# A two-block transformer kernel on one core: state-space products in another order, two tables awaited at first use, and squares ahead of tiles of h

## The reference, cut to what matters

```
# both blocks: mixing and the entry of the feed-forward part
o = merged @ w_out
x = x + g1 * rms_norm(o, g_post_mix)              # second block: x = x + o
h = rms_norm(x, g_pre_ffn) * (1 + sc2) + sh2
f = square(relu(h @ w_ff1)) @ w_ff2
# second block, state-space part, per group of 16 channels with 64 complex states
state[b] = decay * state[b-1] + inputs[b]         # b: blocks of 8 tokens, 128 of them
y[b] = C * state[b-1] + T * u[b]                  # T: lags inside a block of 8 tokens
y = gelu(y)
```

## Time and profile before

| what | us |
|---|---|
| runs: median (lowest to highest) | 3034.39 (3029.42 to 3040.65) |
| the profiled execution's own time | 3021.66 |
| its span, first to last instruction | 3019.9 |
| TensorE busy in the span | 2831.3 |
| VectorE, ScalarE, GpSimd busy | 1938.8, 1307.0, 235.5 |

### The profile page before, as it was taken

The page is one execution under the profiler, slowest core; times in us unless marked ns, Lnnn a source line. Parts: engine busy times, 40 slices in busy tenths (PEclk is TensorE's granted clock), DMA queues, the critical chain, the costliest instruction groups (busy, mean ns, idle before and its releaser), DMA issues. The chain is left out here.

```text
span 3019.9 us, 45306 instructions
## 1 busy us (share of the span) xinstructions
PE 2831.3 (94%) x18392; PEld 2252.8 (75%) x18392; DVE 1938.8 (64%) x2907; ACT 1307.0 (43%) x1908; POOL 235.5 (8%) x427
## 2 busy tenths in 40 slices
PE   7999858898999999989999999998899999999998
PEld 4776734577788788867778788887677888878886
DVE  7768888656776466784777524655646567655676
ACT  3026955457655434453441113222323565543344
POOL 0003620001100000000000001110000010000000
PEclk9999879999999999999999999998999999999999
DMA  7520100235666788731453331114224556667884
GB/s 251 173 84 29 36 1 1 84 112 174 216 224 233 280 259 298 254 120 53 136 161 125 122 110 52 57 48 117 105 91 146 187 196 226 234 247 262 287 296 155
DMA packets 195950, 471.31 MB, mean 156 GB/s; under 512 B 31584, under 2 KB 60384, under 8 KB 189408
## 3 DMA queue, kind: packets, MB, share of 16 engines
q1 hardware_dynamic: 178848, 392.94, 39.4%
q0 software_dynamic: 16896, 75.51, 6.2%
HBM read 344.09 MB, written 124.29 MB: 155 GB/s over the span
## 5 line engine op out<-in xcount | busy, mean ns | idle before, releaser
L2079 PE MATMUL psum<-merged_operand 128*128 128x512 f32 x1536 | 362.5, 391 | 5.8 <-ACT h_half L2332 5.8
L2079 PEld LDWEIGHTS psum<-merged_operand 128*128 128x128 f32 x1536 | 289.4, 188 | 67.6 <-issue 6.6
L2079 PE MATMUL psum<-h_half_operand 128*128 128x512 f32 x1344 | 316.8, 391 | 0.0
L2079 PEld LDWEIGHTS psum<-h_half_operand 128*128 128x128 f32 x1344 | 252.3, 188 | 55.5 <-issue 1.0
L2079 PE MATMUL psum<-h_half_operand,weight_parts_operand 128*128 128x512 f32 x768 | 180.0, 395 | 8.1 <-DVE weight_parts_operand L2564 4.1
L2079 PEld LDWEIGHTS psum<-h_half_operand,weight_parts_operand 128*128 128x128 f32 x768 | 144.5, 189 | 42.7 <-DVE weight_parts_operand L2564 7.3
L235 DVE CAST weight_high<-weight_ring 128x1024 fp32r<-128x1024 f32 (+1 forms) x64 | 37.9, 592 | 196.6 <-PE psum L3508 105.3
L3508 PE MATMUL psum<-h_high,weight_high 128*128 128x512 f32 x480 | 151.8, 397 | 1.4 <-DVE h_low L248 1.4
L3508 PE MATMUL psum<-h_low,weight_high 128*128 128x512 f32 x480 | 148.0, 390 | 0.0
L3508 PE MATMUL psum<-h_high,weight_low 128*128 128x512 f32 x480 | 147.9, 389 | 0.0
L2564 DVE TENSOR_TENSOR weight_parts_operand<-weight_ring,weight_parts_operand 128x1024 fp32r<-128x1024 f32 x66 | 80.7, 1223 | 94.4 <-ACT weight_parts_operand L2228 94.0
(11 more groups left out here) (614 smaller groups left out, 6218.4 us busy)
## 6 DMA issues: line engine op xcount, KB each, us to landing
o<-in_w_ff SPq DMA_DIRECT2D x80, 512.0 KB, 4.5
merged<-hidden_terms SPq DMA_DIRECT2D x56, 512.0 KB, 5.8
hidden_upper<-in_w_ff_down SPq DMA_DIRECT2D x48, 512.0 KB, 4.5
weight_ring<-in_w_out SPq DMA_DIRECT2D x32, 512.0 KB, 3.6
hidden_terms<-weight_parts POOLq DMA_DIRECT2D x16, 1024.0 KB, 7.7
hidden_terms<-weight_ring POOLq DMA_DIRECT2D x16, 1024.0 KB, 7.6
hidden_upper<-in_w_ff_up SPq DMA_DIRECT2D x32, 512.0 KB, 4.6
o<-hidden_terms SPq DMA_DIRECT2D x28, 512.0 KB, 6.0
```

Of the source, the lines that this page charges most:

```text
L2079: mm = pe.matmul(bank, w[:, at:at + P], tiles(r, i), start=opens and m == 0, stop=closes and m == 2, skip_group_check=resumed)
```

## The change

The diff has these parts.

- In `rwkv_output` the landings of `table` and `q` are counted on semaphores of their own; the block's last wait no longer counts them. VectorE waits for `table` ahead of its first use in `ssm_blocks`, TensorE for `q` ahead of its first use.
- The closing `stay_busy` of that block goes from 26 products to 10.
- In `ssm_blocks`, `outputs` becomes `add_inputs` (all products of `u_by_block` with `toeplitz`, opening the sums, ahead of `turn_y` of the four before) and `add_states` (the states' products: first the real parts, then the imaginary parts, each awaited by itself; in each, four of g = 0 and then four of g = 1). ScalarE copies bank 4 after g = 0's last product and bank 5 after g = 1's.
- In mixing with `first`, ScalarE's square of output tile 15 moves ahead of `round_h(5)`, and `keep_p1(0)` ahead of `round_h(6)`; VectorE's additions of squares 14 and 15 move ahead of `scale_first_h(4)` and behind `rest_of_first_h(4)`.
- In both calls `keep_p1(0)` waits for 15 added squares and no longer for 16.

```diff
@@ mix_and_ffn, keep_p1 @@
-                        wait(act, mix_added, MIX)
+                        wait(act, mix_added, MIX - 1 + m)
@@ ScalarE @@
                 if first:
-                    for k in range(4, KT):
-                        round_h(k)
+                    round_h(4)
                 square_output(MIX - 1)
+                if first:
+                    round_h(5)
+                    keep_p1(0)
+                    round_h(6)
+                    round_h(7)
...
-                    if m < PAIRS:
+                    if m < PAIRS and not (first and m == 0):
                         keep_p1(m)
@@ VectorE @@
+                if first:
+                    add_output_square(MIX - 2)
                 for k in range(4 if first else KT, KT):
                     scale_first_h(k)
                     rest_of_first_h(k - 1)
+                    if k == 5:
+                        add_output_square(MIX - 1)
                     if k == 4:
                         rest_of_w(MIX + 1)
                 rest_of_first_h(KT - 1)
                 if not first:
                     rest_of_w(MIX + 1)
                     add_to_x(MIX - 1)
-                add_output_square(MIX - 2)
-                add_output_square(MIX - 1)
+                    add_output_square(MIX - 2)
+                    add_output_square(MIX - 1)
@@ rwkv_output @@
-    LOADS = 4 + 2 * B
+    LOADS = 2 + 2 * B
...
-                sp.dma_start(table, table_dram).then_inc(K.load_done.sem, 16)
-                sp.dma_start(q, q_dram).then_inc(K.load_done.sem, 16)
+                sp.dma_start(table, table_dram).then_inc(landed[2].sem, 16)
+                sp.dma_start(q, q_dram).then_inc(landed[3].sem, 16)
...
-                K.stay_busy(pe, 7, 26)
+                K.stay_busy(pe, 7, 10)
@@ ssm_blocks, VectorE @@
+                    if four == 0:
+                        dve.wait_ge(table_landed.sem, table_landed.n + 16)
                     dve.wait_ge(v_ready, four + 1)
...
-                            c.wait(at["states", four - 1])
+                            c.wait(at["states", four - 1, 1])
...
-                        dve.wait_ge(out_ready, four - 1)
+                        dve.wait_ge(out_ready, 2 * (four - 1))
@@ ssm_blocks, TensorE @@
-                def outputs(four):
-                    pe.wait_ge(K.dve_done.sem, at["states", four])
+                def add_inputs(four):
                     if four == 0:
                         pe.wait_ge(u_copied, 2 * QUADS)
                     else:
                         pe.wait_ge(out_copied, 2 * four)
-                    for i in range(4):
-                        s = 4 * four + i
-                        for o in range(2):
-                            for g in range(2):
-                                rows = slice(g * HD, (g + 1) * HD)
-                                pe.matmul(psum[:, 4 + g, i * P:(i + 1) * P], x[rows, four % 2, o, i, :],
-                                          q[rows, o, s, 1:PW, :].rearrange("p m c -> p (m c)"), start=(o == 0), stop=False)
+                    for g in range(2):
+                        for i in range(4):
+                            pe.matmul(psum[:, 4 + g, i * P:(i + 1) * P], u_t[:, g, 4 * four + i, :],
+                                      toeplitz[:, g, 4 * four + i, :], start=(i == 0), stop=False, skip_group_check=True)
+
+                def add_states(four):
+                    if four == 0:
+                        pe.wait_ge(q_landed.sem, q_landed.n + 16)
+                    for o in range(2):
+                        pe.wait_ge(K.dve_done.sem, at["states", four, o])
                         for g in range(2):
-                            mm = pe.matmul(psum[:, 4 + g, i * P:(i + 1) * P], u_t[:, g, s, :], toeplitz[:, g, s, :],
-                                           start=False, stop=True)
-                    mm.then_inc(out_ready, 1)
+                            rows = slice(g * HD, (g + 1) * HD)
+                            for i in range(4):
+                                mm = pe.matmul(psum[:, 4 + g, i * P:(i + 1) * P], x[rows, four % 2, o, i, :],
+                                               q[rows, o, 4 * four + i, 1:PW, :].rearrange("p m c -> p (m c)"),
+                                               start=False, stop=(o == 1), skip_group_check=True)
+                            if o == 1:
+                                mm.then_inc(out_ready, 1)
...
-                outputs(0)
+                add_inputs(0)
+                add_states(0)
                 state_inputs(3)
                 for four in range(1, QUADS):
+                    add_inputs(four)
                     turn_y(four - 1)
-                    outputs(four)
+                    add_states(four)
@@ ssm_blocks, ScalarE @@
-                    act.wait_ge(out_ready, four + 1)
                     if four >= 2:
                         act.wait_ge(y_turned, 2 * (four - 1))
                     for g in range(2):
+                        act.wait_ge(out_ready, 2 * four + g + 1)
```

More of the change, by code:

```diff
@@ L4454, in rwkv_output @@
         w_low = K.sbuf(ctx, "weight_low", [P, 2, WT * P], F32R)
-        landed = [K.shared_flag(f"landed_{n}") for n in range(2)]
+        landed = [K.shared_flag(f"landed_{n}") for n in range(4)]
         landed0 = [f.n for f in landed]
@@ L4568, in ssm_blocks @@
         at = {}
+        table_landed, q_landed = K.shared_flag("landed_2"), K.shared_flag("landed_3")
         def fours(x):
@@ L4609, in _ @@
                                                  in1=t[:, 2 * o + 1, :, 1:P], op=op))
-                        at["states", four] = c.n
+                        at["states", four, o] = c.n
                 K.dve_done.n = c.n
@@ L4711, in _ @@
                     make_y(four)
+    table_landed.n += 16
+    q_landed.n += 16
 def combine(nc, K, ya, yb, ys, gate, gate_dram):
```

## The result

The changed kernel took 3016.95 us (median of 6 runs, 3011.82 to 3022.95) against 3033.32 us of the kernel before beside it (6 runs): ratio 0.9946, 95% interval 0.9932 to 0.9961. That is 16.4 us less, 11.8 to 20.6. Measured by a threshold of 2% that is "same", as forecast at 0.89, but the interval lies clear of no change.

What follows compares the result with a forecast made beforehand. TensorE was busy 94% of the span, but VectorE bounds `ssm_blocks` up to the last states and ScalarE's queue the first mixing. Gains 3.3 + 2.5 + 2.1 = 7.9 us off median 3034.39 gave 3026.5 us, range 3018 to 3036.

Steps and rivals of the forecast that it cites:

- Landings: End of `rwkv_output`: transfer of `q` and filler both hold the block; taking both away gains 3.3 us.
- VectorE's 40 us: `ssm_blocks` up to the last states: VectorE is the bound at 10.02 us a four and is not shortened.
- D: The moment VectorE ends the last states in `ssm_blocks`, 2175.38 in the execution read; next block at D + 10.95.
- The tail: `ssm_blocks` from last states to next block: 4.2 us gained at full clock, less 1.7 for one fall, leaves 2.5.
- First mixing: ScalarE's queue is what must shorten; moving its work ahead gains 2.1 us, 1.2 with a fall of the clock.
- The sum: All places: 3.3 + 2.5 + 2.1 = 7.9 us, subtracted from the runs' median 3034.39, giving 3026.5.
- No fall, or pairs all the same: `ssm_blocks`' end keeps 4.2 us, 3024.8 in all, or overlapping products save 1.9 more, 3022.9; chance 0.18.
- Gains given back: `ssm_blocks`' end at half clock gains 0.1 us, mixing's 2.1 vanish: 3.4 in all, 3031.0; chance 0.25.
- TensorE becomes the bound: `ssm_blocks`: states' products at half clock take 12.9 us a four, over VectorE's 10.02; 7 us slower, 3041.4; chance 0.05.

Runs made afterwards that it cites:

- the two halves alone: Kernel before with only filler cut to 10, or only `table` and `q` awaited at first use: 3.47 and 3.71 us from VectorE's last multiplication to next block.
- the filler's: Kernel before with only the closing `stay_busy` of `rwkv_output` cut from 26 products to 10: 17.44 us from last states to next block.
- in pairs: Changed kernel with g inside i in the states' products, so g = 0 and g = 1 alternate: 8.80 us from last states to next block.
- the products alone: Kernel before with only the new order of state-space products in `ssm_blocks`: 3025.06 us, ratio 0.9977.
- filling the gap: Changed kernel with g inside i, 12 idle products ahead of last four's states, 8 behind second sum of squares in mixing: 3019.65 us, ratio 0.9954.
- with the gap filled: Kernel before with ten idle TensorE products ahead of the last four's outputs: 9.45 us from last states to next block.

## Why the prediction was wrong, point by point

**Landings: right.** 3.3 predicted, 3.4 seen. The reading that two things hold the block at the same time is shown by the two halves alone. `table` and `q` cost nothing at their first use.

**VectorE's 40 us: right.** From the block's first product to D it is 43.94 to 44.03 us in every run but the filler's. The price that I set for the new states' products was 0.115 us each, at full clock; 2.82 us for 32 make 0.088, and 0.064 in pairs. Products of one row group in a row do cost more, as the Trainium skill's page "TensorE: Matmul & The Clock Gate" (Part 3, The mechanism) led me to hold, but by 0.8 us a four, not by 1.8.

**The tail: the step that failed.** "I therefore charge one fall, 3.4 us at half speed, 1.7 us: **2.5** left." It was mis-sized at both ends. In the new order no half clock met the tail in any of three executions, and the products were 0.8 us faster: 5.97 us where I had 8.4. The wait of 3 us ahead of D, on which the charge rests, was 0.74 to 0.80 us. The clock did fall, but a four earlier, behind a wait of 2.90 to 3.61 us, and was back 2.0 to 2.8 us ahead of D; at half speed the work in between ran beside VectorE's and cost nothing. So the fall is not gone but lies elsewhere, and the run with both states awaited together shows that this can fail. In the kernel before I took 10.95 from one execution, and looked for the clock only to price the new order; it did not occur to me that the row of before held a draw of its own. The mean of the old order's tails without the filler's, whose block began with a fall of its own, is 65.8 / 5 = 13.2. The term was thus 2.5 predicted, 5.0 between the profiled executions, and 7.2 between 13.2 and 5.97; the products alone, timed, gave 7.0 (2.7 to 10.9). The same slip stands in the last sum: I took 7.9 us off the median of the runs as if the execution read and the median had the same tail.

**First mixing: the mechanism right, the choice of clock wrong.** 2.1 predicted without a fall, 1.2 as the bound with one. The changed kernel's profiled execution shows 2.3 without. But in five of the six new-order traces whose gap is not filled the clock fell behind the new wait of 2.03 to 2.05 us; in the changed kernel run again, for one, 0.50 was granted in 698 to 701. Means over the traces, 54.9 old and 53.0 new, leave 1.8 us, and filling the gap brings back 52.35. By itself the part can't be told from nothing in time.

**The sum.** 3.4 + 7.2 + 1.8 = 12.4 us, inside both measured intervals (11.8 to 20.6, and 9.1 to 19.1 for 14.0), and 4 below the 16.4. Another view agrees in kind: 42 executions of before that ran beside the experiments had a mean granted clock of 0.9719, the 15 of the changed kernel 0.975; and within each kernel 0.001 less of it goes with about 2 us more. The profiled pair, with 0.977 and 0.978, was nearly equal in that, and so hid what the change does to the clock. That the whole rest comes from the three places is not shown: ahead of the first of them nothing was changed, and yet the last mixing product ended between 681.06 and 691.58 us over the 14 traces. And the prediction's 15 us, under which a measurement of this kernel can't tell a difference from none, was too much: the interval here is 9 us wide.

**The rivals.** "No fall, or pairs all the same" (3022.9 to 3024.8) was the nearest. "Gains given back" and "TensorE becomes the bound" did not happen: VectorE took 10.0 us a four in all 14 traces, in the shorter filler alone too. Each trace but the two with idle products ahead of the last states shows at least two stretches of half clock between the block's first product and the end of the tail. The rule of the Trainium skill's page "TensorE: Matmul & The Clock Gate" (HAM oscillation) about bursts between waits, which stood beside that last rival, agrees with this in both orders; what differs is whether the second stretch lies ahead of D or behind it.

## What to carry to other kernels

A row that stands behind a wait of TensorE is a draw: before the end of a stage is priced from one trace, ask what it takes at full clock and at half, for the kernel before as for the one after. Moving work from behind the last input to ahead of it gains its own length, here 2.0 us; that it also keeps the clock up is not assured, for here the fall only moved to where another engine was the bound. Where two things end a block together, take both away, and keep TensorE busy until the transfer has landed if only one can go.

## What the runs showed that I had not expected

- 32 instructions of 64 rows take 2.06 us when the two row groups alternate, 2.82 in runs of one group, both at 1.00; the old mixture with 16 of 128 rows took 5.2 for all 48 (D + 0.05 to D + 5.27 with the gap filled), against 2.05 + 2.82 = 4.9 sorted.
- A version whose products are faster (2.06 for 2.82) had the slower tail, 8.80 for 5.97 us, because its fall of the clock lay later; one execution, and not shown to be the pairs' doing.
- Once down, the clock can stay at half while TensorE is busy: with the shorter filler alone from 2172.87 to 2200.18, busy 3.8 to 5.0 us of each 5 from 2175 on.
